# RWKV scan of a two-block decoder: four inverse levels as a TensorE loop, the transposed inverse by VectorE, 96x96 block-diagonal products

## What is computed

```python
def step(S, inp):
    r_t, w_t, k_t, v_t, a_t, b_t = inp
    sa = jnp.einsum("bhij,bhj->bhi", S, a_t)
    S = S * w_t[:, :, None, :] + sa[..., None] * b_t[:, :, None, :] + v_t[..., None] * k_t[:, :, None, :]
    y = jnp.einsum("bhij,bhj->bhi", S, r_t)
    return S, y
S0 = jnp.zeros((B, H, N, N), jnp.float32)
_, ys = lax.scan(step, S0, xs)
```

## Time and profile before

| | us |
|---|---|
| median of 3 runs | 1912.09 |
| lowest, highest | 1902.71, 1918.77 |
| the profiled execution | 1912.39 |
| its span, first to last instruction | 1910.6 |
| mean granted clock of TensorE, share of 2.4 GHz | 0.883 |

### The profile page before, as it was taken

How to read it: one execution, slowest core, us unless ns; L and a number is a source line. 1 busy time by engine, 2 the same in 40 slices (tenths; PEclk the granted TensorE clock), 3 DMA queues, 4 the chain that set the end, 5 groups by cost and what they waited for, 6 DMA issues and landing times.

```text
span 1910.6 us, 44832 instructions
## 1 busy us (share of the span) xinstructions
PE 1702.7 (89%) x18298; PEld 1573.3 (82%) x18298; DVE 838.9 (44%) x1627; ACT 746.7 (39%) x1238; POOL 1099.4 (58%) x554
## 2 busy tenths in 40 slices
PE   7999798557767889999999988989998988979999
PEld 6999798356667789999999976789998864569998
DVE  4333555831213653344333487753346536573300
ACT  5444444311211334445444433544444330454542
POOL 5778586341210457787778761268787530056896
PEclk9999899665666799999999998989999885599999
DMA  5544442000001135455444541045455340023552
GB/s 213 174 161 167 155 153 105 0 4 4 5 4 47 67 132 176 155 167 188 173 169 158 200 138 67 28 145 182 157 183 198 102 169 1 1 92 133 191 202 88
DMA packets 38034, 231.72 MB, mean 121 GB/s; under 512 B 4614, under 2 KB 6759, under 8 KB 16648
## 3 DMA queue, kind: packets, MB, share of 16 engines
q1 hardware_dynamic: 34704, 225.49, 34.1%
q10 hardware_dynamic: 3192, 4.24, 0.7%
HBM read 227.01 MB, written 2.62 MB: 120 GB/s over the span
## 4 chain that ended last, share of the span: by engine, by line
PE 75%; DVE 12%; issue 8%; POOL 3%; ACT 1%; DMA 0%; SPq 0%; DVEq 0%; POOLq 0%; ACTq 0%
PE PS L738 57%; POOL wlo L655 3%; PE PS L995 2%; DVE xl L1495 2%; PE PS L737 1%; PE PS L985 1%; DVE xg L1574 1%; PE PS L872 1%; PE PS L864 1%; DVE ss L1509 1%; PE PS L1004 1%; PE PS L830 1%; PE PS L857 1%; PE PS L812 1%; PE PS L1032 1%
## 5 line engine op out<-in xcount | busy, mean ns | idle before, releaser
L655 POOL TENSOR_TENSOR wlo<-raw,whi 128x1024 fp32r<-128x1024 f32 (+1 forms) x474 | 1035.1, 2206 | 658.6 <-ACT whi L2236 611.3
L738 PE MATMUL PS<-xh,whi 128*128 128x272 f32 (+3 forms) x2392 | 703.2, 294 | 67.3 <-DVE xl L1495 44.2
L738 PE MATMUL PS<-xl,whi 128*128 128x272 f32 (+3 forms) x2392 | 693.1, 290 | 0.0
L738 PE MATMUL PS<-xh,wlo 128*128 128x272 f32 (+3 forms) x2392 | 692.0, 289 | 0.0
L2236 ACT ACTIVATE whi<-raw 128x1024 fp32r<-128x1024 f32 (+1 forms) x474 | 447.8, 977 | 249.2 <-PE PS L738 214.6
L738 PEld LDWEIGHTS PS<-xh,whi 128*128 128x128 f32 (+2 forms) x2392 | 458.4, 192 | 80.0 <-DVE xl L1495 34.3
L738 PEld LDWEIGHTS PS<-xl,whi 128*128 128x128 f32 (+2 forms) x2392 | 460.2, 192 | 0.8
L738 PEld LDWEIGHTS PS<-xh,wlo 128*128 128x128 f32 (+2 forms) x2392 | 460.2, 192 | 0.0
L738 PE MATMUL PS<-hid_h,whi 128*128 128x272 f32 (+1 forms) x960 | 274.0, 285 | 4.9 <-POOL wlo L655 4.9
L738 PE MATMUL PS<-hid_h,wlo 128*128 128x272 f32 (+1 forms) x960 | 273.8, 285 | 0.0
L738 PE MATMUL PS<-hid_l,whi 128*128 128x272 f32 (+1 forms) x960 | 272.8, 284 | 0.0
(11 more groups left out here) (329 smaller groups left out, 1921.5 us busy)
## 6 DMA issues: line engine op xcount, KB each, us to landing
raw<-w_f_in_in SPq DMA_DIRECT2D x88, 1024.0 KB, 4.8
raw<-w_f_dn_in SPq DMA_DIRECT2D x64, 704.0 KB, 4.0
raw<-w_b_ff_in SPq DMA_DIRECT2D x32, 1024.0 KB, 4.7
raw<-w_rk_r_in SPq DMA_DIRECT2D x4, 1024.0 KB, 4.8
raw<-w_rk_k_in SPq DMA_DIRECT2D x4, 1024.0 KB, 4.8
raw<-w_rk_v_in SPq DMA_DIRECT2D x4, 1024.0 KB, 4.9
raw<-w_rk_o_in SPq DMA_DIRECT2D x4, 1024.0 KB, 5.0
raw<-w_at_q_in SPq DMA_DIRECT2D x4, 1024.0 KB, 5.0
```

The costliest lines, as they stand in the source:

```text
L655: nc.gpsimd.tensor_tensor(wlo[U % SPL][:, part], raw[U % RAW][:, part], whi[U % SPL][:, part].bitcast(F32), ALU.subtract).then_inc(s_lo, 1)
L738: mm(out, a, b, start=start and n == 0, stop=stop and n == 2)
```

## The change

- The four levels become one loop of four turns on TensorE; the waits compare with registers. The other engines' code stays written out.
- The inverse is kept in PSUM: `inverse_in` puts it there by a product with the identity, `level_update` adds q x onto it (start=False). Its transpose comes from VectorE (`v.transpose`), which also copies the inverse to SBUF. In the last level VectorE writes the inverse out as 96x96 block-diagonal matrices, by a mask.
- `lak_v`, `uz_product`, the grams of K_, the second part of `transfers` and the first of `inner_parts` become products over 96 rows or onto 96 columns of block-diagonal matrices (6 instead of 18, or 2 + 4 for the grams); VectorE's masks clear what lies outside the 32x32 blocks.
- `masked` becomes `masked_b` and `masked_a`; `lak_v_copy` goes to ScalarE; banks and waits of the gram stage are set anew; the token tiles move to weight buffers.

Left out of the diff: memory layout, semaphore names, the constants' layout.

```diff
+    diag = [np.kron(np.eye(4), x)[:, 0:BLK].astype(np.float32) for x in (strict, incl, np.ones((CH, CH)))]
...
+                def level_mask(p, lv):
+                    tt(tiles32(lm[p][:, :]), tiles32(lt[p][:, :]), mask(2 + lv, 2 * NB), ALU.mult).then_inc(s_lm, 1)
+
                 def inverse_begin(c):
                     p = c % 4
                     pool.wait_ge(s_gr, c + 1)
-                    lt = g4[p][:, :, 0:NB, 0:CH]
                     if c >= 4:
-                        pool.wait_ge(s_gvm, c - 3)
-                    tt(by_block(xb[p][:, 0, :, :]), lt, mask(3, 2, NB), ALU.mult).then_inc(s_pool, 1)
-                    tt(by_block(lm[p][:, :, :]), lt, mask(4, 2, NB), ALU.mult).then_inc(s_lm, 1)
+                        pool.wait_ge(s_yvm, c - 3)
+                    tt(tiles32(xt[p][:, :]), tiles32(lt[p][:, :]), mask(1, 2 * NB), ALU.mult).then_inc(s_pool, 1)
                     pool.wait_ge(s_pool, c + 1)
-                    pool.wait_ge(s_x0, c + 1)
-                    x = xb[p][:, :, :, :].rearrange("p k e (b t) -> p (k e b) t", b=NB)
-                    tt(x, x, mask(8, 4 * NB), ALU.add).then_inc(s_xi, 1)
+                    tt(tiles32(xt[p][:, :]), tiles32(xt[p][:, :]), mask(6, 2 * NB), ALU.add).then_inc(s_xd, 1)
+                    level_mask(p, 0)
 
                 pool.wait_ge(s_rkc, 16)
...
-            def grams(c, s0):
-                for ty, left in enumerate((B_, K_)):
-                    for b, g, e in spread(2):
-                        n = 3 * b + g
-                        mm(PS[gr(g), s0 + e, cols(ty * 192 + b * 64, 64)], left[tk(e), c, cols(n * CH, CH)],
-                           AR[tk(e), c, b, :, gr(g)], start=True, stop=True)
+            def grams_b(c, s0):
                 for b, g, e in spread(2):
                     n = 3 * b + g
-                    last = mm(PS[gr(g), s0 + e, cols(384 + b * CH, CH)], AR[tk(e), c, b, 0, gr(g)],
-                              B_[tk(e), c, cols(n * CH, CH)], start=True, stop=True)
+                    mm(PS[gr(g), s0 + e, cols(192 + b * 64, 64)], B_[tk(e), c, cols(n * CH, CH)], AR[tk(e), c, b, :, gr(g)],
+                       start=True, stop=True)
+                for e in range(2):
+                    last = mm(PS[0:BLK, s0 + e, 0:192], K_[tk(e), c, cols(2 * BLK, BLK)],
+                              AR[tk(e), c, 2, :, :].rearrange("p k t -> p (k t)"), start=True, stop=True)
+                last.then_inc(s_gm, 1)
+
+            def grams_a(c, s0):
+                for b in range(2):
+                    for e in range(2):
+                        last = mm(PS[0:BLK, s0 + e, cols(b * 192, 192)], K_[tk(e), c, cols(b * BLK, BLK)],
+                                  AR[tk(e), c, b, :, :].rearrange("p k t -> p (k t)"), start=True, stop=True)
                 last.then_inc(s_gm, 1)
 
...
             def lak_v(c, s0):
                 p = c % 4
-                pe.wait_ge(s_gr, c + 1)
-                pe.wait_ge(s_tka, 2 * c + 1)
                 for e in range(2):
                     for b in range(NB):
-                        for g in range(3):
-                            last = mm(PS[gr(g), s0 + e, cols(b * 64, 64)], g4[p][gr(g), e, NB + b, 0:CH],
-                                      tok4[p][gr(g), e, b, 2, :], start=True, stop=True)
+                        last = mm(PS[0:BLK, s0 + e, cols(b * 64, 64)], kb[p][:, e, b, 0:BLK], tok4[p][:, e, b, 2, :],
+                                  start=True, stop=True)
                 last.then_inc(s_p1, 1)
 
+            def inverse_in(p):
+                mm(PS[0:BLK, p, 0:192], ident[0:BLK, 0:BLK], xt[p][:, :], start=True, stop=True)
+
             def level_q(p):
-                for e in range(2):
-                    for b in range(NB):
-                        for g in range(3):
-                            last = mm(PS[gr(g), p, cols((NB * e + b) * CH, CH)], lm[p][gr(g), e, cols(b * CH, CH)],
-                                      xb[p][gr(g), 1, e, cols(b * CH, CH)], start=True, stop=True)
+                for n in range(2 * NB):
+                    for g in range(3):
+                        last = mm(PS[gr(g), 4 + p, cols(n * CH, CH)], lm[p][gr(g), cols(n * CH, CH)],
+                                  xx3[p][gr(g), cols(n * CH, CH)], start=True, stop=True)
                 last.then_inc(s_q, 1)
 
-            def level_update(lv, p):
-                for k in range(1 if lv == 3 else 2):
-                    for e in range(2):
-                        for b in range(NB):
-                            for g in range(3):
-                                q, x = qq[p][gr(g), e, cols(b * CH, CH)], xb[p][gr(g), 0, e, cols(b * CH, CH)]
-                                last = mm(PS[gr(g), 4 + p, cols(192 * k + (NB * e + b) * CH, CH)], *((x, q) if k else (q, x)),
-                                          start=True, stop=True)
+            def level_update(p):
+                for n in range(2 * NB):
+                    for g in range(3):
+                        last = mm(PS[gr(g), p, cols(n * CH, CH)], qq[p][gr(g), cols(n * CH, CH)],
+                                  xt[p][gr(g), cols(n * CH, CH)], start=False, stop=True, skip_group_check=True)
                 last.then_inc(s_xt, 1)
 
             def uz_product(c, s0):
                 p = c % 4
                 for e in range(2):
                     for b in range(NB):
-                        for g in range(3):
-                            last = mm(PS[gr(g), s0 + e, cols(b * 128, 128)], xb[p][gr(g), 0, e, cols(b * CH, CH)],
-                                      tok4[p][gr(g), e, b, 0:2, :].rearrange("p k i -> p (k i)"), start=True, stop=True)
+                        last = mm(PS[0:BLK, s0 + e, cols(b * 128, 128)], kb[p][:, e, b, 0:BLK],
+                                  tok4[p][:, e, b, 0:2, :].rearrange("p k i -> p (k i)"), start=True, stop=True)
                 last.then_inc(s_um, 1)
 
...
-                for b, g, e in spread(2):
-                    last = mm(PS[tk(e), g, cols(192 + b * CH, CH)], uz[p][gr(g), e, b, 64:128],
-                              g4[p][gr(g), e, b, CH:2 * CH], start=True, stop=True)
+                for b in range(NB):
+                    for e in range(2):
+                        last = mm(PS[tk(e), 2, cols(192 + b * BLK, BLK)], uz[p][:, e, b, 64:128],
+                                  mrb[p][:, e, cols(b * BLK, BLK)], start=True, stop=True)
                 last.then_inc(s_gvm, 1)
 
             def inner_parts(c):
                 p = c % 4
                 for b in range(NB):
                     for k in range(2):
-                        for g in range(3):
-                            for e in range(2):
-                                left = tok4[p][gr(g), e, b, 2, :] if k else uz[p][gr(g), e, b, 0:64]
-                                mm(PS[tk(e), 3 + g, cols(b * CH, CH)], left, g4[p][gr(g), e, NB * k + b, CH:2 * CH],
-                                   start=k == 0, stop=k == 1)
+                        for e in range(2):
+                            if k:
+                                left, right = tok4[p][:, e, b, 2, :], kb[p][:, e, b, BLK:2 * BLK]
+                            else:
+                                left, right = uz[p][:, e, b, 0:64], mrb[p][:, e, cols(b * BLK, BLK)]
+                            mm(PS[tk(e), 5, cols(192 + b * BLK, BLK)], left, right, start=k == 0, stop=k == 1)
                 for b in range(NB):
                     for k in range(2):
...
-                for lv in range(4):
+                pe.wait_ge(s_gb, c0 + 4)
+                for p in range(4):
+                    pe.wait_ge(s_xd, 16 * half + p + 1)
+                    inverse_in(p)
+                pe.wait_ge(s_p1c, c0 + 4)
+                with link.loop(4, 0) as lv:
                     for p in range(4):
-                        pe.wait_ge(s_lm, 16 * half + 4 * lv + p + 1)
-                        if lv:
-                            pe.wait_ge(s_xd, 16 * half + 4 * (lv - 1) + p + 1)
-                        else:
-                            pe.wait_ge(s_xi, c0 + p + 1)
-                            if p == 2:
-                                pe.wait_ge(s_x0, c0 + 4)
+                        pe.wait_ge(s_lm, val(16 * half + p + 1, lv, 4))
+                        pe.wait_ge(s_xx, val(16 * half + p + 1, lv, 4))
+                        pe.nop(nofuse=True)
                         level_q(p)
                     for p in range(4):
-                        pe.wait_ge(s_qc, 16 * half + 4 * lv + p + 1)
-                        if lv == 0:
-                            pe.wait_ge(s_p1c, c0 + (3, 3, 4, 4)[p])
-                        level_update(lv, p)
-                pe.wait_ge(s_xd, 16 * half + 13)
-                uz_product(c0, 0)
-                pe.wait_ge(s_xd, 16 * half + 16)
+                        pe.wait_ge(s_qc, val(16 * half + p + 1, lv, 4))
+                        pe.wait_ge(s_xd, val(16 * half + p + 1, lv, 4))
+                        pe.nop(nofuse=True)
```

(70 more changed lines are left out.)

145 lines of the change are left out of this document (76 added, 69 removed).

## The result

The changed kernel took 1840.72 us in the median of four runs (1833.55 to 1843.07), the kernel before 1914.8 beside it; the ratio is 0.9617, with a 95% interval from 0.9564 to 0.967. The forecast was 1869, with a range from 1845 to 1893, so the direction was right, the size was not, and the range missed the time at its fast end. The profiled execution took 1843.07 us against 1912.4, which is 69.3 less, and all of it lies in the scan.

The account below looks back on a forecast made before the run. The scan's levels were taken as bound by instruction feeding, one block of 256 per 3.73 us. Gram +2.5, levels -42.6 and transfers -3.0 sum to -43.1, so 1912.4 us becomes 1869, range 1845 to 1893.

Parts of the forecast that it names:

- What bound the kernel: Scan levels: TensorE is fed one block of 256 instructions per 3.73 us; instruction count, not arithmetic, is the bound.
- The body stays in the engine: Levels loop: about 630 instructions a turn are not fetched anew after the first turn; stage 24.9 us instead of 46.4 and 46.0.
- rival C: Levels: the body does not stay, each turn takes 9.1 us, the stage 37; 1893 us in all; chance 0.08.
- rival D: Levels: the body does not stay and fetches do not overlap with execution, 14.3 us a turn; 1934 us; chance 0.04.
- Turn 1 at 2.45 x 3.73 = 9.1 us: Levels: the loop's first turn, 2.45 blocks of instructions, is fed at 3.73 us per block, 9.1 us.
- Turns 3 and 4 at 5.13 us, at half clock: Levels: each turn after the first executes 288 pairs at 17.8 ns, 5.13 us.
- rival B: Levels and transfers: without gaps TensorE is granted 2.4 GHz, a turn about 3.4 us; 1840 us; chance 0.16, whole or half.
- The 0.4 us a half for branches: Levels: 0.4 us added to each stage for the loop's branches and first waits.
- Transfers 37.5 and 33 us: Transfers stages: 37.5 us against 38.5 in the first half, 33 against 35.1 in the second; sum -3.
- rival E: Wide products of the two heads do not overlap: 24 us more, and some 5 in the gram stages; 1898 us; chance 0.09.
- Gram stages +2.5 us: Gram stages: 20.1 us against 18.8 and 20.6 against 19.3, put at 2.5 us more for both.
- its own range, 1856 to 1886: Whole kernel: the forecast's range from gram +2.5 to +12, levels -38 to -43, transfers -10 to +5.

Follow-up runs that it names:

- run 1: The changed kernel with the four levels written out on TensorE instead of looped: 1878.94 us, ratio 0.9821.
- run 2: The kernel before with its four levels as a loop on TensorE, both products computed in every turn: 1875.46 us, ratio 0.9788.
- run 5: The changed kernel with two levels in the loop's body and two turns: 1853.31 us (one time).
- run 10: The kernel of run 4 with the products of inverse_in made five times over: 1844.07 us (one time).
- run 4: The changed kernel with VectorE's additions and ScalarE's copies of K_ and the state put ahead of the uz copies in the transfers: 1819.11 us, ratio 0.9507.
- run 6: The kernel of run 4 with 128 empty instructions on TensorE in front of the scan: 1818.0 us (one time).

## Why the forecast was wrong, step by step

**What bound the kernel: right.** The levels were bound by the feeding of instructions. Run 1 (9 blocks in 32.4 us) and run 2 (less time with more instructions) show it.

**The body stays in the engine: right.** There is no instruction wait and no transfer on the instruction queue in turns 2 to 4 here, and no instruction wait in the second turn of run 5. Behind that measurement: the Trainium skill (Runtime: NRT & Kernel Launch, Instruction fetch mechanics) gives TensorE room for 2048 instructions, and bodies of some 630 and 1240 agree with it (none above that was run); its rule that a branch out of a window of two pages waits for a fetch shows nowhere in these loops. Rivals C and D fell with that.

**Turn 1 at 2.45 x 3.73 = 9.1 us: wrong, 6.0 and 6.6 measured.** This is the first term that failed, worth 5.6 us. The period of 3.73 us was used as a rate for any number of instructions. But the waits stand only at block ends, and after a stage that is not fed at its limit (344 pairs in 19.2 us) the engine seems to have a block in hand: the turn contains two ends (387 and 514 pairs from the scan's start) and stops at one, in run 10 at a later one. That block in hand is an inference, not shown. In run 2, where the gram stage before it is itself at the limit, the period does hold as a rate for the first turn: its 864 matmul and load instructions alone are 3.4 blocks, 12.6 us, and 12.4 were measured (with the others, some 930 in all, it would be 13.6).

**Turns 3 and 4 at 5.13 us, at half clock: wrong, 3.7 and 3.4 measured.** The second failed term, 6.4 us over both halves. The forecast named the case (rival B, a turn of 3.4 us) and gave it 0.16, because the clock read 0.50 "even where 127 pairs ran without a gap". Those 127 pairs lasted 2.5 us and had a wait on each side. Run 2 shows the same products at full clock once the waits are gone. Turn 2 was right: 5.3 and 5.1 us at 0.57 and 0.61. The 0.4 us a half for branches was not seen, and the finer edges of the stages give the last 1.2 of the 13.9 us.

**Transfers 37.5 and 33 us: wrong, 30.2 and 27.8 measured.** This third failed term is worth 12 us. Three errors lie in it. The four instruction waits of 1 us do not exist: there are none. The work at half clock was set too short: 33.5 us without instruction waits, where run 1's second half takes 37.6 at 0.50, 1.1 of it the wait ahead of the serial pass, and has none; one chunk with its stop takes 10.1 us here, not 9.3, as 12 pairs of uz_product are 2.88, not 2.6, the 64-column products 1.54 and 0.87, not 1.3 and 0.67. These two cancel but for about 1 us. What remains, 6 to 7 and 5 us, is the clock again, 0.65 and 0.78. The stops for VectorE (1.76 forecast as 1.78) and the 96-column products (12 in 1.01 us, 85 ns each as forecast) were right, so rival E fell: the heads' products do overlap.

**Gram stages +2.5 us: nearly right, +1.2.** VectorE's cadence for a chunk is 3.67 us against 3.6 to 3.7. The transpose costs 372 ns, in the bounds of 350 to 950 and at the value taken; the copy 315. The 1.5 us a half for instruction waits did not come; lak_v took 1.07 us, not 0.7. The 16.6 us to the last lak_v were met (16.7), though the sum as written (3.0, four times 3.6 to 3.7, less 0.35) gives 17.1 to 17.5: the 0.6 us behind the last chunk has to be left out as well.

**The sum.** 12.7 + 1.2 us in the levels, 11.8 in the transfers and 1.3 in the gram stages make the 27 us between -43.1 and -70.1. The levels' 6.4 and most of the transfers' rest have one cause, a clock taken from the kernel before as if it belonged to the stage; it rose when the waits went (runs 2 and 4) and fell when they came back (run 1). Instruction waits that were counted where none came make most of the other part. The number of rival B, 1840, was met by luck: B had its parts otherwise, 9.1 us for turn 1 and 26 for the transfers. Two slips in the forecast carried nothing: its own range, 1856 to 1886, is 1862 to 1891 by the bounds that it names, and the 132 pairs fewer with uz are 96 (252 to 156).

Still open is why turn 2 stays at half clock for most of its length, why the same levels run at 0.67 in one execution and at 0.90 in another (runs 4 and 6), and why waits like those of the levels went with full clock in the gram stage of the kernel before.
